# Expert weights of a mixture-of-experts layer issued as their pages fall free, the first reload in four steps, the last second weights in two parts

## The reference

```python
g_p, g_idx = lax.top_k(g_prob, 1)                    # one of 4 groups for a token
e_p, e_idx = lax.top_k(softmax(e_sel), 2)            # two of its 8 experts
y = (silu(hb @ w1[e]) * (hb @ w3[e])) @ w2[e]        # w1, w3: 1024x512, w2: 512x1024
x = x + g2 * sum over the two experts of gate * y
return rmsnorm(x, final_g)
```

## Time and profile before

| | |
|---|---|
| median of 3 runs | 1435.38 us (1432.23 to 1435.62) |
| profiled execution: time, span | 1428.55 us, 1426.8 us |
| PE busy | 1204.0 us (84%) |
| expert weights: first issue, last product's end | 931.2 us, 1416.6 us |
| DMA between 1000 and 1300 us | 428 GB/s, all 16 DMA engines busy |
| PE in the same 300 us | 176 us busy |

### The profile page before, as it was taken

One profiled execution on the slowest core, in us unless ns is written; L12 is line 12 of the kernel. 1 busy time (PEld: TensorE's weight loads), 2 busy tenths in 40 slices (PEclk: granted clock), 3 DMA queues, 4 the chain that ended last, 5 costly groups with the idle time before them and its releaser, 6 DMA issues.

```text
span 1426.8 us, 19205 instructions
## 1 busy us (share of the span) xinstructions
PE 1204.0 (84%) x8218; PEld 874.7 (61%) x8218; DVE 591.9 (41%) x968; ACT 435.8 (31%) x688; POOL 16.1 (1%) x32
## 2 busy tenths in 40 slices
PE   5999989999999999999999989898573575746677
PEld 5998766699887787599988677645131221312222
DVE  4678414576543767276642558722010100101001
ACT  4653320444333685254433513531000010000001
POOL 3000000000000000000000000000000000000000
PEclk9999989999999999999999999999886877868899
DMA  8352659355554553245554633089999999999995
GB/s 268 132 191 105 214 204 352 129 187 188 205 185 154 195 208 144 82 163 187 196 199 148 224 107 129 1 365 400 429 427 429 428 427 428 430 428 428 427 429 203
DMA packets 98353, 363.04 MB, mean 254 GB/s; under 512 B 7226, under 2 KB 10645, under 8 KB 86373
## 3 DMA queue, kind: packets, MB, share of 16 engines
q1 hardware_dynamic: 96240, 357.70, 64.6%
q0 software_dynamic: 1680, 4.10, 1.0%
q10 hardware_dynamic: 356, 0.13, 0.1%
HBM read 360.87 MB, written 1.05 MB: 254 GB/s over the span
## 4 chain that ended last, share of the span: by engine, by line
PE 61%; DMA 21%; DVE 5%; ACT 3%; issue 2%; SPq 1%; DVEq 0%; ACTq 0%
PE bank L918 33%; DMA arena<-in_exp_w 21%; PE bank L626 7%; PE bank L1032 3%; PE bank L1560 2%; DVE arena L2218 2%; PE bank L890 2%; PE bank L1225 2%; PE bank L857 2%; PE bank L703 2%; PE bank L900 1%; SPq L2811 1%; PE bank L1242 1%; PE bank L1270 1%; PE bank L1256 1%
## 5 line engine op out<-in xcount | busy, mean ns | idle before, releaser
L626 PE MATMUL bank<-arena 128*32 128x512 f32 x880 | 185.6, 679 | 74.7 <-DMA arena<-in_exp_w 73.8
L1723 DVE TENSOR_TENSOR low_w<-ring,split_high 128x2048 fp32r<-128x2048 f32 x84 | 189.5, 2289 | 104.0 <-ACT split_high L2412 104.0
L918 PE MATMUL bank<-turned_high,low_w 128*128 128x256 f32 x720 | 204.4, 284 | 0.0
L2412 ACT ACTIVATE split_high<-ring 128x2048 fp32r<-128x2048 f32 x84 | 157.8, 1916 | 136.6 <-DMA ring<-in_w_down 67.9
L626 PE MATMUL bank<-ring,arena 128*32 128x512 f32 x528 | 95.3, 703 | 83.0 <-DMA arena<-in_exp_w 83.0
L918 PE MATMUL bank<-turned_high,split_high 128*128 128x256 f32 x512 | 145.8, 285 | 3.0 <-DVE turned_low L1738 3.0
L918 PE MATMUL bank<-turned_low,split_high 128*128 128x256 f32 x512 | 144.9, 283 | 0.0
L918 PEld LDWEIGHTS bank<-turned_high,low_w 128*128 128x128 f32 x720 | 138.9, 193 | 0.0
L626 PEld LDWEIGHTS bank<-arena 128*32 128x32 f32 x880 | 48.6, 123 | 134.1 <-issue 134.1
L772 DVE TENSOR_TENSOR arena<-arena,bank 128x512 f32<-128x512 f32 x8 | 5.5, 688 | 298.9 <-PE bank L626 256.3
L626 PEld LDWEIGHTS bank<-ring,arena 128*32 128x32 f32 x528 | 27.3, 127 | 147.5 <-issue 147.5
(11 more groups left out here) (451 smaller groups left out, 1937.2 us busy)
## 6 DMA issues: line engine op xcount, KB each, us to landing
arena<-in_exp_w SPq DMA_DIRECT2D x59, 2048.0 KB, 23.2
ring<-in_exp_w SPq DMA_DIRECT2D x33, 2048.0 KB, 20.0
ring<-in_w_up SPq DMA_DIRECT2D x16, 2048.0 KB, 9.1
ring<-in_w_down SPq DMA_DIRECT2D x16, 2048.0 KB, 7.8
ring<-in_mod_w SPq DMA_DIRECT2D x12, 2048.0 KB, 8.9
ring<-in_w_in_ar SPq DMA_DIRECT2D x7, 2048.0 KB, 8.5
ring<-in_w_qkv SPq DMA_DIRECT2D x6, 2048.0 KB, 8.1
ring<-in_ple_gate SPq DMA_DIRECT2D x4, 2048.0 KB, 8.4
```

Of the source, the lines that this page charges most:

```text
L626: last = nc.tensor.matmul(mb[bank][strip(e), :], act[:, k, strip(e)], w[e][:, k, cols], start=(k == 0), stop=(k == n_k - 1), skip_group_ch ...
L918: last = mm(dst, *pair, start=(start and i == 0), stop=(stop and i == 2))
L1723: v.tensor_tensor(low_of(name, s), half_of(slot(name), name, s), high_of(name, s).bitcast(F32), ALU.subtract).then_inc(sem("split_low"), 1)
L2412: nc.scalar.activation(high_of(name, s), half_of(slot(name), name, s), ACT.Copy)\
```

## The change

Six edits, all for the experts.

1. The DMA scratch of POOL is cut from its default 16 KiB to 4 KiB a partition. The room, with the small buffers `mod_sum` and `cond_strips`, makes a buffer `spare` of 16 KiB, and the constants are laid out anew so that two pairs of tables that are read early form places of 4 KiB. `early_place` goes from 6 to 11 pieces; five are left for late loading.
2. SP issues four pieces right behind the last half of `w_out2`, then units and pieces as the arena's pages fall free in the attention: 1 (after `poolo` and `qabs`), 0, two pieces, 2 and 3, and only then 4 after the attention's weights are read.
3. The first product raises `pair_read` after each two k but the last. After each, SP loads one row block m of the four w2 of group 0 as four pieces; the last four follow `moe_full[0]`. Before, four whole units were issued after `moe_full[0]`.
4. The four w3 of the last group are loaded as eight halves, first k = 0 to 3 of all experts, then k = 4 to 7. The product goes over k outside and experts inside, in two parts, each behind its own wait.
5. `last_products` takes the m that have all their pieces early first: 2, 3, then 0, 1.
6. The last scatter raises `moe_sum` for each bank and not for each two; ACT squares the first bank and scales it before it waits for the second.

The diff, cut to its core:

```diff
-        early_place = {(2, 2): page(25), (2, 3): const[:, table_at:table_at + D], (3, 0): hT[:, 0:D],
-                       (3, 1): hT[:, D:2 * D], (3, 2): x3[:, 0, :], (3, 3): x3[:, 1, :]}
+        early_place = {(1, 1): const[:, masks_at:masks_at + D], (1, 2): spare[:, D:2 * D], (1, 3): spare[:, 2 * D:3 * D],
+                       (2, 0): spare[:, 3 * D:4 * D], (2, 1): spare[:, 0:D], (2, 2): const[:, keys_at:keys_at + D],
+                       (2, 3): page(25), (3, 0): hT[:, 0:D], (3, 1): hT[:, D:2 * D], (3, 2): x3[:, 0, :],
+                       (3, 3): x3[:, 1, :]}
...
+                if by_pairs and k % 2 and k < n_k - 1:
+                    last.then_inc(sem("pair_read"), 1)
...
+                order = sorted(range(EC), key=lambda m: len(late_of[m]) > 0)
+                for m in order:
...
-                for e in range(IN_GROUP):
-                    at = unit + IN_GROUP + e
-                    w = blocks(moe_slot[unit_slot(at)], KC)
-                    pe.wait_ge(moe_landed[unit_slot(at)], unit_landed(turn, at))
-                    for k in range(KC):
-                        done = mm(mb[1][strip(e), :], gathered_k[:, k, strip(e)], w[:, k, :], start=(k == 0),
-                                  stop=(k == KC - 1), skip_group_check=True)
+                for part in range(2):
+                    if part:
+                        pe.wait_ge(sem("moe_late_landed"), 16 * IN_GROUP * EC)
+                    else:
+                        for e in range(IN_GROUP):
+                            pe.wait_ge(moe_landed[unit_slot(at + e)], unit_landed(turn, at + e))
+                    for k in range(part * KC // 2, (part + 1) * KC // 2):
+                        for e in range(IN_GROUP):
+                            done = mm(mb[1][strip(e), :], gathered_k[:, k, strip(e)], w[e][:, k, :], start=(k == 0),
+                                      stop=(k == KC - 1), skip_group_check=True)
...
             for t in range(NT):
-                act.wait_ge(sem("moe_sum"), t + 1)
                 for n in range(2):
+                    act.wait_ge(sem("moe_sum"), 2 * t + n + 1)
...
+            load_early((1, 1), (1, 2), (1, 3), (2, 0))
+            sp.wait_ge(sem("pool_ready"), 1)
+            for g in range(2):
+                banks.read(sp, "poolo", g)
+            for g in range(4):
+                banks.read(sp, "qabs", g)
+            load_unit(0, 1)
+            sp.wait_ge(sem("rel_used"), 8)
+            load_unit(0, 0)
+            banks.read(sp, "mod_rows_first")
+            load_early((2, 1))
+            banks.wait_read(sp, "dsa", "s", 0)
+            load_early((2, 2))
+            banks.read(sp, "dsa", "s", 2 * HEADS - 1)
+            load_unit(0, 2)
+            banks.wait_read(sp, "dsa", "s", 2 * HEADS - 1)
+            banks.read(sp, "dsa", "pT", 2 * HEADS - 1)
+            load_unit(0, 3)
             sp.wait_ge(*unit_read[("dsa",)])
-            for i in range(5):
-                load_unit(0, i)
+            load_unit(0, 4)
...
+                for m in range(EC):
+                    if m < EC - 1:
+                        sp.wait_ge(sem("pair_read"), m + 1)
+                    else:
+                        sp.wait_ge(moe_full[0], filled(0, 0, FIRST))
+                    for e in range(IN_GROUP):
+                        at = unit_slot(MOE_SLOTS + e)
+                        src = sources[2][e].rearrange("(p k) n -> p k n", p=P)
+                        sp.dma_start(blocks(moe_slot[at], EC)[:, m, :], src[:, m, :])\
+                            .then_inc(sem("moe_late_landed") if m < EC - 1 else moe_landed[at], 16)
...
+                sp.wait_ge(moe_full[3], filled(2 * GROUPS_A_TURN * turns, 0, SECOND))
+                for part in range(2):
+                    for e in range(IN_GROUP):
+                        load_half(part, e)
...
-    nc = bacc.Bacc("TRN2", target_bir_lowering=False, num_devices=1)
+    nc = bacc.Bacc("TRN2", target_bir_lowering=False, num_devices=1, dynamic_dma_scratch_size=4096)
```

More of the change, by code:

```diff
@@ L54 @@
 CONST_WIDTHS = [
-    ("ident", P), ("eps", 1), ("ln_eps", 1), ("level", P * len(LEVELS)), ("strict", P), ("upto", P), ("ones", P), ("pairs", P),
+    ("ident", P), ("eps", 1), ("ln_eps", 1), ("level", P * len(LEVELS)), ("pairs", P), ("strict", P), ("upto", P), ("ones", P),
     ("cos", NT * 64), ("sin", NT * 64), ("causal", S), ("allowed", NT * S), ("pool_inv", 2 * S),
-    ("first", 8), ("iota", SLOTS_OF), ("zero", P), ("mod_sel", MOD_UNITS),
+    ("first", 8), ("iota", SLOTS_OF), ("mod_sel", MOD_UNITS),
 ]
@@ L391, in build @@
         cqT = blocks(half(10), 2)
-        ckvT, ckv_tok = page(5)[:, 512:768], blocks(page(5)[:, 768:1024], NT)
+        ckvT, ckv_tok = half(49)[:, 0:256], blocks(half(49)[:, 256:512], NT)
         qiT = blocks(page(6), 4)
@@ L617, in choose, with group_products @@
             last.then_inc(sem("selected"), 1)
-        def group_products(pe, bank, turn, unit, act, n_k, cols):
+        def group_products(pe, bank, turn, unit, act, n_k, cols, by_pairs=False):
             w = [blocks(moe_slot[unit_slot(unit + e)], n_k) for e in range(IN_GROUP)]
@@ L633, in first_products @@
                 pe.wait_ge(moe_freed[bank], filled(turn * (2 * GROUPS_A_TURN), q, FIRST) - 1)
-                group_products(pe, bank, turn, unit + IN_GROUP * bank, gathered_k, KC, slice(0, 512))
+                group_products(pe, bank, turn, unit + IN_GROUP * bank, gathered_k, KC, slice(0, 512),
+                               by_pairs=(at_start and bank == 0))
         def sparse_pe(pe, y_bank):
@@ L647, in scatter @@
                                   start=False, stop=last, skip_group_check=True)
[L648 to L649 removed]
+                        if last:
+                            done.then_inc(sem("moe_sum"), 1)
             def last_products(turn, unit):
[L653 to L654 removed]
+                late_of = {m: [e for e in range(IN_GROUP) if (m, e) not in early_place] for m in range(EC)}
+                order = sorted(range(EC), key=lambda m: len(late_of[m]) > 0)
+                for m in order:
+                    late = late_of[m]
                     if late:
@@ L2813, in load_unit, with load_half, load_piece, load_early @@
                     .then_inc(moe_landed[unit_slot(i)], 16)
+            def load_half(part, e):
+                at, ks = unit_slot(a_turn - 2 * IN_GROUP + e), slice(part * KC // 2, (part + 1) * KC // 2)
+                sp.dma_start(blocks(moe_slot[at], KC)[:, ks, :], pkn(sources[1][N_EXP - IN_GROUP + e])[:, ks, :])\
+                    .then_inc(moe_landed[at] if part == 0 else sem("moe_late_landed"), 16)
+            def load_piece(m, e, place, landed_as):
+                src = sources[2][N_EXP - IN_GROUP + e].rearrange("(p k) n -> p k n", p=P)
+                sp.dma_start(place, src[:, m, :]).then_inc(sem(landed_as), 16)
+            def load_early(*pieces):
+                for at in pieces:
+                    load_piece(*at, early_place[at], "early_landed")
+            load_early((1, 1), (1, 2), (1, 3), (2, 0))
[16 more added lines that the diff above has]
+            load_unit(0, 3)
             sp.wait_ge(*unit_read[("dsa",)])
-            for i in range(5):
-                load_unit(0, i)
+            load_unit(0, 4)
             for c in range(2):
```

57 lines of the change are left out of this document (29 added, 28 removed).

## The result

| | before | changed |
|---|---|---|
| median (lowest to highest) | 1433.81 us (1430.04 to 1435.62, 4 runs) | 1418.03 us (1415.82 to 1420.15, 4 runs) |
| profiled execution, span | 1428.55, 1426.8 us | 1419.30, 1417.5 us |

The ratio is 0.9898, 95% interval 0.9875 to 0.9921. The forecast, 1425.6 us and a range of 1419.5 to 1432, had the direction right, and the time lies 1.5 us under the range.

A forecast was written before the change was run, and what follows sets the result against it. It took the kernel's last 470 us as bound by moving 201 MB of expert weights, then TensorE alone. Gains of 3.7, 5.2 and 0.86 us, 9.8 in all, off the median gave 1425.6 us; whole range 1419.5 to 1432.

The forecast's parts named there:

- the last of the sum: Final step: take the summed gain of 9.8 us off the shown runs' median, 6.8 us above the profiled execution, giving 1425.6.
- The stream: Expert weight loading from the second group on: 5.3 us earlier start less 1.6 us for small pieces, 3.7 us ahead.
- The start: First reload's issue at 974.5 us, SP past its branch in time, data at 976.2 against 981.5: 5.3 us earlier.
- the sixteen pieces: First reload as small transfers instead of four units: 1.0 to 2.7 us dearer, taken as 1.6 us.
- The end: After the last w1 product: two-part w3 product gains 5.2 us, ACT's earlier start after the scatter 0.86 us.
- Part two: Second half of the last w3 product, after 6.5 us idle: 3.44 us plus 2.2 us for lost clock, 5.65 us.
- the eight slow products of the chain: Products read as following 7 us or more of idle time, 8.46 to 10.03 us, mean 9.3; basis of the 2.2 us clock term.
- Edits at nothing: Terms put at 0 us, among them waits for late pieces, zero products' operands, the moved page and POOL's smaller scratch.
- The earlier issue gives nothing: Rival for the stream's start: the 3.7 us are lost, gain 6.1 us, time 1429.3; chance 0.10.
- Each small transfer pays its start: Rival: sixteen more transfers each pay 1.66 us unhidden, 26.6 us, so 16.8 us slower, 1452; chance 0.06.
- The clock is lost at the end: Rival: part two throughout and half the w2 product at half clock; gain 5.1 us, 1430.3; chance 0.14.
- All at full rate, clock kept: Rival: pieces and halves at full rate and no clock loss; gain 14.0 us, 1421.4; chance 0.10.

The follow-up runs named there:

- `before`: The unchanged kernel, in its first profiled execution: 1428.55 us; median beside the changed kernel 1433.81 us.
- `before_again`: The unchanged kernel run once more beside itself: median 1430.79 us, ratio 0.9989.
- `tail_only`: The kernel before with edits 4, 5 and 6 alone, six early pieces as before: median 1422.6 us, ratio to before 0.9934.
- `batch`: Changed kernel with the first reload's first twelve pieces as three 2 MiB transfers and the four second halves as one of 4 MiB: 1419.56 us, ratio to before 0.9922.
- `late_issue`: Changed kernel with all units and pieces issued only after the attention's last read, reload in four steps and eleven early pieces kept: 1429.7 us, ratio to before 0.9995.
- `best`: Changed kernel with the merged 2 and 4 MiB transfers plus six zero products between the last w3 product's two parts: 1415.48 us, ratio to before 0.989.
- `no_halves`: Changed kernel with edit 4 undone, last w3 as four whole units and product expert by expert: 1426.88 us, ratio to before 0.9967.
- `after_third`: The changed kernel unaltered, third trace, run once more beside `best`: median 1421.33 us, ratio to before 0.9936.

## Why the prediction was wrong

**The step that failed** is the last of the sum: "so I put the gain of 9.8 us to the median". The gain was near; the base was not. All 73 runs of the kernel before (its 12 runs under its own label among them) have a median of 1431.05 and a mean of 1430.8 us; all 22 of the changed kernel have 1419.9 and 1420.0. The means differ by 10.8 us, 95% interval 9.1 to 12.5, and 9.8 lies in it. The interval takes all runs as independent; by session the difference of the means is 15.3, 12.6 and 9.2 us. Counted from 1431.05 the same gain would have forecast 1421.3, 1.3 us from the pooled 1419.9. Of the 7.6 us between 1425.6 and 1418.03, 4.3 come from the base (1435.38 - 1431.05), 1.9 from four quick runs of the changed kernel (1419.9 - 1418.03), and 1.3 are left for the gain. The profiled execution, 6.8 us under the three runs, was a hint that three runs don't fix the base. I saw it, and read it as a fixed offset of the profiled execution; it was the spread of single runs, 1423.0 to 1436.9. The range should have taken in a base some 4 us lower. That a good part of the spread is there by 280 us and goes with the granted clock is shown by the twelve traces above; as much again arises between there and F. Why the clock differs from run to run stays open.

**The stream: forecast 3.7, measured 4.65.** The mean of L - F is 403.9 before and 399.25 after. The start was right: SP was not late at its branch, and the reload came where it was put. The sum speaks of the lead "from the second group on", and there it was right: G is at F + 50.5 in the three traces with the old start (`before`, `before_again`, `tail_only`) and at F + 46.6 in the mean of the changed kernel's three, 3.85 us earlier. In the span that is 1020.5 against 1023.06, since F was 1.25 us later. If the start is 5.3 us earlier, as the sum has it, the sixteen pieces cost 1.45 us; I took 1.6, and `batch`, which merges twelve of them, gets 1 us back at this point. The other 0.8 us arise later, mostly between F + 66 and F + 150, where the products of the traces with the old start fall behind their step of 19.6 us by 0.6 to 1.2 us in all and the changed kernel's by 0.0 to 0.35. I had no term for this. `late_issue`, `batch` and `best` lose 0.5 to 0.6 us there too. The cause stays open; in steps of 4 us the DMA rate does not fall below 410 GB/s there in the three traces with the old start, so it is not a hole.

**The end: forecast 5.2 + 0.86, measured 5.95.** The mean of E - L is 51.25 before and 45.3 after. Undoing the halves costs 5.2 us against two traces and 4.4 against all three. That 5.2 is the forecast to the digit is luck in part: the last w1 product of `no_halves` happened to take 8.5 us, as in the trace that I counted from. ACT's 0.86 stands in the rows, but no run has edit 6 alone. Part two was put at 5.65 us and took 5.22 to 6.29 in the seven traces without zero products. One thing the sum had (1380.9 against 1382.45) and did not say: in the changed kernel the last w1 product is off the path, since part one waits for its halves 0.6 to 1.0 us after it is over. Before, a slow clock in that product was paid in full; it took 8.46 us in the first trace and 9.97 in the second, which is why their E - L are 50.5 and 52.0. One reading was wrong: of the eight slow products of the chain seven come after 7 us or more of idle time; the one at 1180.42 came after 2.68 us. The mean of the seven is 9.4 us and not 9.3, which changes the term by 0.1 us.

**Edits at nothing.** The w2 pieces were never waited for, the late ones have landed by 1399 us, ahead of the w2 product at 1401.06. The attention lost nothing that can be told from its spread. POOL's smaller scratch costs nothing that shows: the chain comes to its 2.08 us product near 147 us at 146.7 to 147.5 us in the three traces with the default scratch and at 146.4 to 147.7 in the nine with 4 KiB. SP's sixteen pieces took 9.99 us to issue with no one waiting behind.

**The rivals.** "The earlier issue gives nothing" is refuted by the 3.9 us of the pairs. "Each small transfer pays its start" is refuted by `batch`: nine transfers fewer in the first reload gave 1 us and not 9 x 1.66 = 15. "The clock is lost at the end" is half true: part two began at half clock in all seven traces without zero products, but never ran at it throughout (6.9 us), and the w2 product lost 1.7 us in 2 of 9 traces of this form of the end. "All at full rate, clock kept" came nearest in time with 1421.4, by luck: the pieces were not at full rate, the clock was not kept, and its gain of 14.0 us is outside 9.1 to 12.5. Counted from 1431.05 it would be 1417.1, further from the pooled 1419.9 than the forecast's 1421.3.

## What to carry to other kernels

A sum of microseconds is as good as the base that it is taken from. When the profiled execution and the timed runs differ by half the expected gain, treat the base as unknown by that much, and judge the change from a point in the trace that both kernels share to the end, not from the whole time. A transfer issued early pays only if what stands behind it is issued early too: here the early issue alone gave 0.7 us, both together 4.65, and the reload in steps without it gave nothing in the one run that bears on it.

## What the runs showed of the hardware

- The granted clock fell to 0.50 in an idle gap of 6.2 us, and part two of the w3 product took 5.22 to 6.29 us instead of 3.64, 1.6 to 2.7 us more. With zero products in the gap it stayed at full clock (3.64 us in two traces).
- In the twelve traces, 48 products of four strips that had waited 1.12 to 2.37 us for a DMA all took 7.07 or 7.08 us. Of 28 that had waited 2.39 to 3.18 us, 27 took 8.71 to 8.78 us and one, after 2.60 us, 7.07. After 6.17 us or more all took 8.36 to 10.04 us.
- Gaps of some 0.95 and 0.69 us around the four transposes ahead of the w2 product were followed by 0.50 in two traces (`after_third`, `best`) and not in the other ten. The Trainium skill (TensorE: Matmul & The Clock Gate, under What's actually happening) says that the gate's timing does not start anew with a kernel. No run here shows that timing itself; that equal gaps cost in one run and not in another would fit it.
- The same dense work, all of it ahead of 280 us, took up to 7.6 us more or less in twelve executions (6.3 us between two of the changed kernel), at a granted clock of 0.86 to 1.00 in 200 to 250 us.
- From 976 us on, behind the hole, pieces of 512 KiB moved at 139, 350, 358, 385 and 387 GB/s in stretches of 2 us before they reached 416; transfers of 2 MiB, from 974 us on, at 158, 401 and 420.
- With the queue full, one issue of a piece took SP 3.97 us, two together 8.53, and sixteen in a row 20.44 us, against 9.99 us for sixteen on a queue that had run empty.
